# PEER value stage on one Trainium2 core: value unit and up-unit multiplied in turn, weights split in that order

## The chip, the cores and the metric

One Trainium2 chip, one of its cores. The metric is the device time of one execution in microseconds; the lower the better. TensorE does the matrix products, VectorE (DVE) and ScalarE (ACT) the elementwise work, GpSimd (POOL) a little of it, and the queue of SyncE (SP) starts the weight loads.

## What is computed

Two blocks of layers over 256 tokens of width 1024, all in float32. The change touches only the last part of each of the two layers of the second block, the PEER layer, a mixture of 16384 small experts:

```python
def peer_ffn(h, w_query, sub_keys, expert_u, expert_v):
    ...
    expert_idx = jnp.take_along_axis(cand_idx, pos, axis=-1)
    gates = jax.nn.softmax(best, axis=-1).astype(h.dtype)
    ...
    def block(args):
        xb, idx, g = args
        u = expert_u[idx]
        a = jax.nn.gelu(jnp.einsum('tkd,td->tk', u, xb)) * g
        return jnp.einsum('tk,tkd->td', a, expert_v[idx])
```

The kernel computes it densely: gelu(u·h) for all 16384 experts, times a gate matrix that is zero where an expert was not chosen, times v.

## The kernel before

**Tiles.** `expert_u` and `expert_v` are cut into 64 pairs each; a pair is one load of 1 MB and holds two units of 128 experts (128 partitions by 1024). An *up-unit* u(n,0), u(n,1) of pair n is multiplied by `project`: for each of 8 slices of 128 columns, three matmuls with the weight slice stationary and the 256 tokens moving (`triple`, L606 to L608), so 24 matmuls of 256 columns. A *value unit* v(n,0), v(n,1) takes 12 matmuls of 512 columns (`loose`, L611 to L613): stationary is a slice of the activation, moving is half of the weight unit; they add into four banks `acc[0..3]` over all 128 value units. There are three matmuls for each product because float32 is kept by splitting both factors: `w_hi` (rounded by ACT, L1145) and `w_lo = raw - w_hi` (by DVE, L1604), and likewise `p_hi` (ACT, L1539) and `p_lo` (DVE, L2176) for the activation.

**Buffers.** `raw` has three slots of one pair (NRAW = 3). `w_hi` and `w_lo` have four slots of one unit (NPAIR = 4): unit number g goes into slot g % 4, so ACT may split unit g only when TensorE has done unit g - 4 (semaphore `used`, in the trace a wait on L613 or L608). The numbers of the units follow `weight_order`, and every engine takes them in that order.

**Order.** NPAIRS = 33: when the value stage begins, 33 of the 64 up-pairs are done. Step n of the stage (n = 0..30) multiplies v(n,0), v(n,1) and then u(n+33,0), u(n+33,1); from n = 31 a step has value units only. In each step the other engines do, strictly in this order:
- ACT: gelu of up-pair n+32 (L1467, it frees a PSUM bank and needs the last up-unit of step n-1), `products(n+1)`, that is `p_hi` twice (L1539), every fourth step the load of a chunk of gates, and then four splits L1145.
- DVE: `products(n+1)`, that is the product with the gates (L2172, called the gate product below), which releases `p_hi`, and `p_lo` twice (L2176); then the four splits L1604.

```python
                        for e2 in range(2):
                            w_hi_upto(unit[("peer_v", l), 2 * n + e2] + NPAIR)
...
            def pair(key, n):
                w_hi_upto(unit[key, 2 * n + 1] + NPAIR)
```

With the unit numbers before, the four splits of step n are u(n+33,1), v(n+1,0), v(n+1,1), u(n+34,0). SP loads a pair when the last unit in its `raw` slot is split on DVE.

Of the kernel before, what the change touches and what calls it, by code (L numbers as in the profile page):

```python
# [17 lines left out]
T = 256  # L18
# [6 lines left out]
NRAW = 3  # L25
NPAIR = 4
# [85 lines left out]
def weight_order(a):  # L112

    order, first, n = [], {}, 0

    def add(key, src, count, lo="v", n0=0):
        nonlocal n
        for i in range(n0, n0 + count):
            first.setdefault(key, n) if n0 == 0 and i == 0 else None
            order.append((src[i], lo, n))  # L120
            place[key, 2 * i], place[key, 2 * i + 1] = n, n + 1
            n += 2

    place = {}
    for l in range(L):
        add(("ffn1_gu", l), a["ffn1_gu"][l], 22)
        add(("ffn1_down", l), a["ffn1_down"][l], 11)
        add(("w_in", l), a["w_in"][l], 8)
        add(("w_v", l), a["w_v"][l], 2)
        add(("w_out", l), a["w_out"][l], 4)  # L130
        add(("ffn2_gu", l), a["ffn2_gu"][l], 22)
        add(("ffn2_down", l), a["ffn2_down"][l], 11)
    spread, n_ada, seen = [], 0, 0
    for i, entry in enumerate(order):
        spread.append(entry)
        seen += not 33 <= i % 80 < 50
        while n_ada < 48 and n_ada < (seen - 2) * 48 // 122:
            spread.append((a["ada_w_2"][n_ada // 24][n_ada % 24], "ada", n_ada))
            n_ada += 1
    assert n_ada == 48  # L140
    order[:] = spread

    def add_peer(l):
        u, v = a["peer_u"][l], a["peer_v"][l]
        for i in range(8):
            add(("peer_q", l), a["peer_q"][l], 1, "v" if i < 2 else "p", i)
            if i >= 1:
                add(("peer_u", l), u, 1, "v" if i == 1 else "p", i - 1)
        add(("peer_u", l), u, NPOOL - 7, "p", 7)
        add(("peer_u", l), u, NPAIRS - NPOOL, "v", NPOOL)  # L150
        for i in range(64):
            add(("peer_v", l), v, 1, "v", i)
            if i + NPAIRS < 64:
                add(("peer_u", l), u, 1, "v", i + NPAIRS)

    add("ret_qk", a["ret_qk"], 8)
    add("ret_v", a["ret_v"], 8)
    add("ret_g", a["ret_g"], 8)
    add("ret_out", a["ret_out"], 8)
    add_peer(0)  # L160
    add("sgu_v", a["sgu_v"], 12)
    add("sgu_u", a["sgu_u"], 12)
    add("sgu_out", a["sgu_out"], 12)
    add_peer(1)
    return order, place, n


def build(nc, a, out):
    ctx = ExitStack()
    with ctx:  # L170
# [61 lines left out]
        hi_done = signal("w_hi_done", lambda n: n + 1)  # L232
        lo_count, ada_n, halves = {"v": 0, "p": 0}, 0, []
        lo_key = {}
        for k, (src, lo, n) in enumerate(order):
            for half in range(2):
                if lo == "ada":
                    halves.append((k, half, lo, 2 * n + half))
                else:
                    halves.append((k, half, lo, n + half))  # L240
                    lo_count[lo] += 1
                    lo_key[n + half] = (lo, lo_count[lo])
        w_lo_dve = signal("w_lo_done_dve", lambda n: lo_key[n][1])
        w_lo_pool = signal("w_lo_done_pool", lambda n: lo_key[n][1])
        lo_done = {"v": w_lo_dve, "p": w_lo_pool}
# [10 lines left out]
        class Banks:  # L256
# [3 lines left out]
            def take(self, key):  # L260
                self.at = (self.at + 1) % len(self.ids)
                i = self.ids[self.at]
                before, held[i] = held.get(i), key
                bank[key] = psum[i]
                return psum[i], before
# [336 lines left out]
        def _(e):  # L602
# [411 lines left out]
            def peer(l):  # L1014
# [14 lines left out]
                def u_pair(n):  # L1029
                    u_unit(2 * n)  # L1030
                    u_unit(2 * n + 1)
# [6 lines left out]
                def key_scores(n):  # L1038
# [7 lines left out]
                                         keys[:, 2 * n + z, :], start=True, stop=True)  # L1046
                    t.then_inc(psc_done.hit(l, n), 1)

                project_pairs(q, ("peer_q", l), 0, outs)
                for n in range(1, 8):  # L1050
                    if n > 1:
# [35 lines left out]
                for k in range(4):  # L1087
                    held[4 + k] = ("acc", l, k)
                w.wait_ge(*row_read(q))
                for n in range(64):  # L1090
                    for e2, ks in ((0, range(4)), (1, range(4))) if n < 63 else ((0, (0, 1)), (1, (0, 1)), (0, (2, 3)), (1, (2, 3))):
                        u = 2 * n + e2
                        g = unit[("peer_v", l), u]
                        wh, wl = weights(g)
                        i = u % 4
                        w.wait_ge(p_lo_done, p_lo_done(l, u))
                        for k in ks:
                            c, tt = slice(k // 2 * 512, (k // 2 + 1) * 512), slice(k % 2 * 128, (k % 2 + 1) * 128)
                            t = loose(acc[k], (p_hi[i][:, tt], p_lo[i][:, tt]), (wh[:, c], wl[:, c]), u == 0, u == 127)
                            if u == 127 and k < 3:  # L1100
                                t.then_inc(acc_done.hit(l, k), 1)
                        if ks[-1] == 3:
                            t.then_inc(used.hit(g), 1)
                    if n + NPAIRS < 64:
                        u_pair(n + NPAIRS)
                for m in range(KT):
                    if m % 2 == 0:
                        w.wait_ge(*free_after(held[m // 2]))
# [23 lines left out]
        def _(e):  # L1132
# [314 lines left out]
            def peer(l):  # L1447
# [97 lines left out]
                for n in range(64):  # L1545
                    if n < 63:
                        products(n + 1)
                        for e2 in range(2):
                            w_hi_upto(unit[("peer_v", l), 2 * n + e2] + NPAIR)
                    if n == 48:  # L1550
                        ready_root(3 + l)
                    if n + NPAIRS < 64:
                        u_pair(n + NPAIRS)
# [34 lines left out]
        def _(e):  # L1588
# [450 lines left out]
            def peer(l):  # L2039
# [140 lines left out]
                for n in range(64):  # L2180
                    if n < 63:
                        products(n + 1)
                        for e2 in range(2):
                            w_lo_upto(unit[("peer_v", l), 2 * n + e2] + NPAIR)
                    if n + NPAIRS < 64:
                        pair(("peer_u", l), n + NPAIRS)
                w.wait_ge(*unit_after(("peer_v", l), 127))
# [82 lines left out]
        @block.sync  # L2270
        def _(e):
            w = Waits(e)
            for k, (src, lo, n) in enumerate(order):
                if k == 0:
                    e.dma_start(raw_t[:, 0, 0:UNIT], src[:, 0:UNIT]).then_inc(raw_first.sem, 16)
                    e.dma_start(cols[:, 0:8], a["cols"][:, 0:8]).then_inc(loads["gain"].sem, 16)
                    w.wait_ge(raw_first, 16)
                    e.dma_start(raw_t[:, 0, UNIT:2 * UNIT], src[:, UNIT:2 * UNIT]).then_inc(landed[0].sem, 16)
                    continue
                if k < NRAW:  # L2280
                    w.wait_ge(*((loads["x2"], 16) if k == 1 else (landed[0], 16)))
                elif k >= NRAW:
                    _, before, m = order[k - NRAW]
                    if before == "ada":
                        w.wait_ge(ada_done, ada_done(2 * m + 1))
                    else:
                        w.wait_ge(lo_done[before], lo_key[m + 1][1])
                e.dma_start(raw_t[:, k % NRAW, :], src).then_inc(landed[k % NRAW].sem, 16)
                if k == 2:
                    e.dma_start(ident, a["ident"]).then_inc(loads["ident"].sem, 16)  # L2290
                    e.dma_start(iof, a["iota"]).then_inc(loads["iota"].sem, 16)
                    e.dma_start(crow, a["c_2"].partition_broadcast(128)).then_inc(loads["c"].sem, 16)
                    e.dma_start(relb, a["rel_bias"]).then_inc(loads["relb"].sem, 16)
                    e.dma_start(oh, a["onehot"]).then_inc(loads["oh"].sem, 16)
                    e.dma_start(anti, a["anti"]).then_inc(loads["anti"].sem, 16)
                    e.dma_start(half1, a["half1"]).then_inc(loads["half"].sem, 16)
                for l in range(L):
                    if n == unit[("peer_u", l), 2 * NPAIRS] and lo != "ada":
                        for i in range(2):
                            w.wait_ge(g_stored[i], 128 * (l + 1))  # L2300
                    for c in range(4):
                        if n == unit[("peer_u", l), 2 * (NPAIRS + c)] and lo != "ada":
                            e.dma_start(G[c], gates[l, :, :, c * 128:(c + 1) * 128].rearrange("g p c -> p g c")).then_inc(g_read[c].sem, 16)
            for m in range(KT):
                w.wait_ge(fin_ready, fin_ready(m))
                e.dma_start(out[:, m, :], fin[:, m, :]).then_inc(stored.sem, 16)
            w.wait_ge(stored, 16 * KT)
            w.wait_ge(bias_out, 16)
# [127 lines left out]
```

## Time and profile before

| | |
|---|---|
| median of 3 runs | 3047.86 us (3041.24 to 3049.73) |
| span of the profiled execution | 3041.1 us |
| TensorE busy | 3019.4 us, 99% of the span |
| DVE, ACT busy | 72%, 53% |
| granted clock of TensorE over the span | 0.997 |

The profile shows one execution, whose own time is given as its span; it lies 0.1 us under the fastest of the three runs and 6.8 us under their median. In the trace TensorE's matmuls overlap (each is shown for its whole way through the array), so the cost of one is the distance from its start to the next start, not its duration.

### The profile page before, as it was taken

How to read it: one execution, taken by the hardware profiler on the slowest of the kernel's cores; microseconds unless marked ns; L12 is line 12 of the kernel's file. 1: busy time of each engine (PE TensorE's matmuls, PEld its weight loads, DVE VectorE, ACT ScalarE, POOL GpSimd, SP SyncE). 2: the span in 40 equal slices, each digit the busy share in tenths (PEclk: the TensorE clock that was granted, in tenths of full speed). 3: DMA queues.
4: the chain of work that ended last, by engine and by line, in shares of the span. 5: the costliest groups of instructions: out<-in, count | busy, mean ns of one | idle time of the engine just before them, and what ended most of it. 6: DMA issues, size and time to landing. Idle time of an engine off the chain costs nothing.

```text
span 3041.1 us, 53499 instructions
## 1 busy us (share of the span) xinstructions
PE 3019.4 (99%) x22650; PEld 2849.6 (94%) x22650; DVE 2184.3 (72%) x3459; ACT 1615.1 (53%) x2399; POOL 255.2 (8%) x233
## 2 busy tenths in 40 slices
PE   9999999999999999999999999999999999999999
PEld 9998999999999999999999998889999999999887
DVE  6877787876788756899555557776679975555676
ACT  5565554565554455556544445556445564444554
POOL 0010001010001001820000000000146000000000
PEclk9999999999999999999999999999999999999999
DMA  7762577774277545557856667555445687666663
GB/s 258 267 248 96 195 277 256 273 275 167 102 258 290 173 146 180 178 180 291 296 206 214 216 212 245 208 190 191 163 170 181 229 302 249 218 213 216 222 235 125
DMA packets 153693, 654.61 MB, mean 215 GB/s; under 512 B 10508, under 2 KB 77648, under 8 KB 78960
## 3 DMA queue, kind: packets, MB, share of 16 engines
q1 hardware_dynamic: 97744, 584.99, 54.1%
q10 hardware_dynamic: 55296, 64.76, 6.3%
q8 instruction: 179, 2.93, 0.4%
q0 software_dynamic: 416, 1.45, 0.1%
q14 instruction: 58, 0.48, 0.0%
HBM read 616.55 MB, written 34.61 MB: 214 GB/s over the span
## 4 chain that ended last, share of the span: by engine, by line
PE 92%; DVE 6%; ACT 1%; issue 0%; DMA 0%; DVEq 0%; ACTq 0%
PE ps L606 18%; PE ps L607 18%; PE ps L608 18%; PE ps L612 8%; PE ps L613 8%; PE ps L611 8%; PE ps L1074 2%; PE ps L801 2%; DVE w_lo L1604 2%; PE ps L678 1%; PE ps L681 1%; PE ps L679 1%; PE ps L663 1%; PE ps L657 1%; PE ps L658 1%; PE ps L693 1%
## 5 line engine op out<-in xcount | busy, mean ns | idle before, releaser
L1604 DVE TENSOR_TENSOR w_lo<-raw,w_hi 128x1024 fp32r<-128x1024 f32 x933 | 1139.5, 1228 | 588.6 <-ACT w_hi L1145 587.6
L1145 ACT ACTIVATE w_hi<-raw 128x1024 fp32r<-128x1024 f32 x1000 | 1050.5, 1055 | 658.0 <-PE ps L608 357.1
L606 PE MATMUL ps<-h_hi,w_hi 128*128 128x256 f32 x4240 | 1188.6, 280 | 5.0 <-DVE w_lo L1604 3.4
L607 PE MATMUL ps<-h_lo,w_hi 128*128 128x256 f32 x4240 | 1179.1, 278 | 0.0
L608 PE MATMUL ps<-h_hi,w_lo 128*128 128x256 f32 x4240 | 1179.0, 278 | 0.0
L606 PEld LDWEIGHTS ps<-h_hi,w_hi 128*128 128x128 f32 x4240 | 797.1, 188 | 10.8 <-issue 4.1
L608 PEld LDWEIGHTS ps<-h_hi,w_lo 128*128 128x128 f32 x4240 | 802.2, 189 | 0.0
L607 PEld LDWEIGHTS ps<-h_lo,w_hi 128*128 128x128 f32 x4240 | 796.4, 188 | 2.8 <-issue 0.2
L613 PE MATMUL ps<-w_hi,at 128*128 128x512 f32 x1024 | 398.4, 389 | 0.0
L612 PE MATMUL ps<-w_lo,at 128*128 128x512 f32 x1024 | 398.4, 389 | 0.0
L611 PE MATMUL ps<-w_hi,at 128*128 128x512 f32 x1024 | 398.4, 389 | 0.0
L606 PE MATMUL ps<-at,w_hi 128*128 128x256 f32 x1024 | 284.2, 278 | 2.2 <-DVE w_lo L1604 1.8
L608 PE MATMUL ps<-at,w_lo 128*128 128x256 f32 x1024 | 283.7, 277 | 0.0
L607 PE MATMUL ps<-at,w_hi 128*128 128x256 f32 x1024 | 283.7, 277 | 0.0
L613 PEld LDWEIGHTS ps<-w_hi,at 128*128 128x128 f32 x1024 | 192.3, 188 | 39.7
L611 PEld LDWEIGHTS ps<-w_hi,at 128*128 128x128 f32 x1024 | 192.3, 188 | 37.5
L612 PEld LDWEIGHTS ps<-w_lo,at 128*128 128x128 f32 x1024 | 192.1, 188 | 37.6
L606 PEld LDWEIGHTS ps<-at,w_hi 128*128 128x128 f32 x1024 | 192.9, 188 | 2.9 <-issue 2.0
L608 PEld LDWEIGHTS ps<-at,w_lo 128*128 128x128 f32 x1024 | 192.4, 188 | 0.0
L607 PEld LDWEIGHTS ps<-at,w_hi 128*128 128x128 f32 x1024 | 192.2, 188 | 0.0
L2244 POOL TENSOR_TENSOR tmp_h<-x 128x256 f32<-128x256 f32 x50 | 36.8, 736 | 1842.0 <-DVE x L1649 1717.8
L1467 ACT ACTIVATE at<-ps 128x512 f32<-128x512 f32 x128 | 76.7, 599 | 201.5 <-PE ps L608 201.5
(287 smaller groups left out, 3210.6 us busy)
## 6 DMA issues: line engine op xcount, KB each, us to landing
raw<-in_peer_u SPq DMA_DIRECT2D x128, 1024.0 KB, 4.8
raw<-in_peer_v SPq DMA_DIRECT2D x128, 1024.0 KB, 4.8
raw<-in_ffn_gu SPq DMA_DIRECT2D x87, 1024.0 KB, 4.9
raw<-in_ada_w SPq DMA_DIRECT2D x48, 1024.0 KB, 5.1
raw<-in_ffn_down SPq DMA_DIRECT2D x44, 1024.0 KB, 4.9
gates<-at ACTq DMA_DIRECT2D x32, 1024.0 KB, 4.9
at<-gates ACTq DMA_DIRECT2D x24, 1024.0 KB, 6.0
raw<-in_w_in SPq DMA_DIRECT2D x16, 1024.0 KB, 4.9
```

Of the source, the lines that this page charges most:

```text
L606: e.matmul(o, lhs[0], rhs[0], start=start, stop=False)
L607: e.matmul(o, lhs[0], rhs[1], start=False, stop=False)
L608: return e.matmul(o, lhs[1], rhs[0], start=False, stop=stop)
L611: e.matmul(o, lhs[0], rhs[0], start=start, stop=False, skip_group_check=True)
L612: e.matmul(o, lhs[0], rhs[1], start=False, stop=False, skip_group_check=True)
L613: return e.matmul(o, lhs[1], rhs[0], start=False, stop=stop, skip_group_check=True)
L801: t = e.matmul(conv.bank[:, i * T:(i + 1) * T], mdiag[:, n, :], mu_[:, 2 + i, k:k + T], start=k == 0, stop=k == 30)
L1074: t = e.matmul(b[:, k * 128:(k + 1) * 128], Ah[j][:, z, :, 4 * i + k], Bh[j][:, 2 * i + k // 2, :, k % 2], start=z == 0, stop=z == 1)
L1145: e.activation(whi[:, u % NPAIR, :], raw(k, half), ACT.Copy).then_inc(hi_done.hit(u), 1)
L1467: e.activation(R[:, i:i + 2, :].rearrange("p a b -> p (a b)"), bank["u", l, n], ACT.Gelu_apprx_tanh).then_inc(u_done.hit(l, n), 1)
L1604: e.tensor_tensor(wlo[:, m % NPAIR, :], raw(k, half), whi[:, m % NPAIR, :].bitcast(FP), ALU.subtract).then_inc(w_lo_dve.hit(m), 1)
L2244: t = e.tensor_tensor(one if m else total, x[:, m, :], x[:, m, :], ALU.mult)
```

## The change

In steps 0 to 30 a value unit and an up-unit of the same half are multiplied in turn: `values_and_unit(n, e2)` issues one matmul of 512 columns, two of 256, and so on, 12 and 24 of them; then the same for the other half. The units are numbered v(n,0), u(n+33,0), v(n,1), u(n+33,1), and are split in that order. Steps 31 to 63 stay. The matmuls are the same in number and shape. The load of a pair now waits for the split of the unit two numbers after the pair's first (`m + last`).

```diff
+    def add_two(key, src, i, key2, src2, i2):
+        nonlocal n
+        for z, (ky, s, j) in enumerate(((key, src, i), (key2, src2, i2))):
+            order.append((s[j], "v", n + z, 2))
+            place[ky, 2 * j], place[ky, 2 * j + 1] = n + z, n + z + 2
+        n += 4
...
-        for i in range(64):
-            add(("peer_v", l), v, 1, "v", i)
-            if i + NPAIRS < 64:
-                add(("peer_u", l), u, 1, "v", i + NPAIRS)
+        for i in range(64 - NPAIRS):
+            add_two(("peer_v", l), v, i, ("peer_u", l), u, i + NPAIRS)
+        add(("peer_v", l), v, 64 - (64 - NPAIRS), "v", 64 - NPAIRS)
...
+                def values_and_unit(n, e2):
+                    v, u = 2 * n + e2, 2 * (n + NPAIRS) + e2
+                    gv, gu = unit[("peer_v", l), v], unit[("peer_u", l), u]
+                    i, s = v % 4, slice(e2 * T, (e2 + 1) * T)
+                    if e2 == 0:
+                        u_bank[0] = take(ub, ("u", l, n + NPAIRS))
+                    o = u_bank[0][:, s]
+                    vh, vl = weights(gv)
+                    w.wait_ge(p_lo_done, p_lo_done(l, v))
+                    uh, ul = weights(gu)
+                    for k in range(4):
+                        c, tt = slice(k // 2 * 512, (k // 2 + 1) * 512), slice(k % 2 * 128, (k % 2 + 1) * 128)
+                        a_, b_ = 2 * k, 2 * k + 1
+                        ca, cb = slice(a_ * 128, (a_ + 1) * 128), slice(b_ * 128, (b_ + 1) * 128)
+                        e.matmul(acc[k], p_hi[i][:, tt], vh[:, c], start=v == 0, stop=False, skip_group_check=True)
+                        e.matmul(o, uh[:, ca], hh_[:, a_, :], start=k == 0, stop=False, skip_group_check=True)
+                        e.matmul(o, uh[:, ca], hl_[:, a_, :], start=False, stop=False, skip_group_check=True)
+                        e.matmul(acc[k], p_hi[i][:, tt], vl[:, c], start=False, stop=False, skip_group_check=True)
+                        e.matmul(o, ul[:, ca], hh_[:, a_, :], start=False, stop=False, skip_group_check=True)
+                        e.matmul(o, uh[:, cb], hh_[:, b_, :], start=False, stop=False, skip_group_check=True)
+                        t = e.matmul(acc[k], p_lo[i][:, tt], vh[:, c], start=False, stop=False, skip_group_check=True)
+                        if k == 3:
+                            t.then_inc(used.hit(gv), 1)
+                        e.matmul(o, uh[:, cb], hl_[:, b_, :], start=False, stop=False, skip_group_check=True)
+                        t = e.matmul(o, ul[:, cb], hh_[:, b_, :], start=False, stop=k == 3, skip_group_check=True)
+                    t.then_inc(used.hit(gu), 1)
...
-                for n in range(64):
+                for n in range(64 - NPAIRS):
+                    for e2 in range(2):
+                        values_and_unit(n, e2)
+                for n in range(64 - NPAIRS, 64):
...
-                        for e2 in range(2):
-                            w_hi_upto(unit[("peer_v", l), 2 * n + e2] + NPAIR)
+                        if n + NPAIRS >= 64:
+                            w_hi_upto(unit[("peer_v", l), 2 * n + 1] + NPAIR)
...
-                        w.wait_ge(lo_done[before], lo_key[m + 1][1])
+                        w.wait_ge(lo_done[before], lo_key[m + last][1])
```

On TensorE, at the first value step of the first PEER layer, the rows before are these (`ps1` is the bank of the up-pair, `ps4` to `ps7` are `acc`, the `at` tiles are `p_hi` and `p_lo`):

```order
L606 MATMUL ps0<-h_hi,w_hi 128x256
L607 MATMUL ps0<-h_lo,w_hi 128x256
L608 MATMUL ps0<-h_hi,w_lo 128x256
L611 MATMUL ps4<-w_hi,at29456_229_230 128x512 [waits n_scaled,w_lo_done_dve,G_ready,p_lo_done]
L612 MATMUL ps4<-w_lo,at29456_229_230 128x512
L613 MATMUL ps4<-w_hi,at30480_237_238 128x512
L611 MATMUL ps5<-w_hi,at29456_229_230 128x512
L612 MATMUL ps5<-w_lo,at29456_229_230 128x512
```

and with the change these, ending where the second half's group begins:

```order
L1074 MATMUL ps7<-w_hi,at29456_229_230 128x512
L1075 MATMUL ps1<-h_hi,w_hi 128x256
L1076 MATMUL ps1<-h_lo,w_hi 128x256
L1077 MATMUL ps7<-w_lo,at29456_229_230 128x512
L1078 MATMUL ps1<-h_hi,w_lo 128x256
L1079 MATMUL ps1<-h_hi,w_hi 128x256
L1080 MATMUL ps7<-w_hi,at30480_237_238 128x512
L1083 MATMUL ps1<-h_lo,w_hi 128x256
L1084 MATMUL ps1<-h_hi,w_lo 128x256
L1074 MATMUL ps4<-w_hi,at29712_231_232 128x512 [waits w_lo_done_dve,p_lo_done]
```

A group of 36 matmuls has one wait at its head, for the split of both of its units, where before each unit waited for its own. The value unit's slot is given back by L1080, the third matmul from the group's end, and the up-unit's by the last.

On ACT, one whole step before (gelu, `p_hi` twice, four splits, the next gelu):

```order
L1467 ACTIVATE at12544_225_226<-ps0 128x512 [waits p_lo_done,w_used]
L1539 ACTIVATE at29968_233_234<-at12544_225_226 128x256 [waits rg_mul]
L1539 ACTIVATE at30224_235_236<-at12544_225_226 128x256
L1145 ACTIVATE w_hi<-raw 128x1024
L1145 ACTIVATE w_hi<-raw 128x1024 [waits w_used,raw_landed2]
L1145 ACTIVATE w_hi<-raw 128x1024 [waits w_used]
L1145 ACTIVATE w_hi<-raw 128x1024 [waits w_used,raw_landed0]
L1467 ACTIVATE at12544_225_226<-ps1 128x512 [waits p_lo_done,w_used]
```

and the same step with the change:

```order
L1506 ACTIVATE at12544_225_226<-ps0 128x512 [waits p_lo_done,w_used]
L1578 ACTIVATE at29968_233_234<-at12544_225_226 128x256 [waits rg_mul]
L1578 ACTIVATE at30224_235_236<-at12544_225_226 128x256
L1184 ACTIVATE w_hi<-raw 128x1024
L1184 ACTIVATE w_hi<-raw 128x1024 [waits w_used,raw_landed2]
L1184 ACTIVATE w_hi<-raw 128x1024 [waits w_used,raw_landed0]
L1184 ACTIVATE w_hi<-raw 128x1024 [waits w_used]
L1506 ACTIVATE at12544_225_226<-ps1 128x512 [waits p_lo_done,w_used]
```

The four splits were u(n+33,1), v(n+1,0), v(n+1,1), u(n+34,0) and are now u(n+33,1), v(n+1,0), u(n+34,0), v(n+1,1): the wait for a new up-pair (`raw_landed0`) moves one place forward, and the last split before gelu is that of a value unit of the second half.

DVE's rows are the same in both, with the four splits in the new order of units:

```order
L2211 TENSOR_TENSOR at12544_225_226<-at12544_225_226,at4096_273_274 128x512 [waits u_done]
L2215 TENSOR_TENSOR at30992_241_242<-at12544_225_226,at29968_233_234 128x256 [waits p_hi_done]
L2215 TENSOR_TENSOR at31248_243_244<-at12544_225_226,at30224_235_236 128x256 [waits p_hi_done]
L1643 TENSOR_TENSOR w_lo<-raw,w_hi 128x1024 [waits w_hi_done] x4
L2211 TENSOR_TENSOR at12544_225_226<-at12544_225_226,at6144_275_276 128x512 [waits g_read3,u_done]
```

The last of the four splits (`x4`), now v(n+1,1), stands ahead of the next gate product in this queue.

## Rows read from the trace of the kernel before

**Rows 1.** The page: span, busy time by engine, chain that ended last.

```profile
span 3041.1 us, 53499 instructions
PE 3019.4 (99%) x22650; PEld 2849.6 (94%) x22650; DVE 2184.3 (72%) x3459; ACT 1615.1 (53%) x2399; POOL 255.2 (8%) x233
...
PE 92%; DVE 6%; ACT 1%; issue 0%; DMA 0%; DVEq 0%; ACTq 0%
```

**Rows 2.** Busy time, clock and DMA share of a value step.

```profile
core 0: us, PE busy (x) PEld busy (x) DVE busy (x) ACT busy (x) POOL busy (x), PEclk, DMA share, GB/s
1688.50:1699.59 11.09, 11.09 (x74) 10.15 (x73) 6.26 (x8) 5.34 (x7) 0.00 (x0) 1.00 0.86 283
```

**Rows 3.** Timeline of TensorE, one value step: start, us, what.

```profile
1499.93 0.39 PE L611 MATMUL ps<-w_hi,at 128*128 128x512 f32 x1
...
1505.37 0.28 PE L606 MATMUL ps<-h_hi,w_hi 128*128 128x256 f32 x1
1505.49 0.28 PE L607 MATMUL ps<-h_lo,w_hi 128*128 128x256 f32 x1
...
1511.03 0.39 PE L611 MATMUL ps<-w_hi,at 128*128 128x512 f32 x1
```

**Rows 4.** Timeline of TensorE ahead of the value stage, up-units alone.

```profile
1461.07 0.28 PE L606 MATMUL ps<-h_hi,w_hi 128*128 128x256 f32 x1
...
1466.51 0.28 PE L606 MATMUL ps<-h_hi,w_hi 128*128 128x256 f32 x1
```

**Rows 5.** Timeline of TensorE, end of a value unit.

```profile
1604.98 0.39 PE L613 MATMUL ps<-w_hi,at 128*128 128x512 f32 x1
1605.21 0.28 PE L606 MATMUL ps<-h_hi,w_hi 128*128 128x256 f32 x1
```

**Rows 6.** Timeline of ACT, one value step.

```profile
1599.97 0.60 ACT L1467 ACTIVATE at<-ps 128x512 f32<-128x512 f32 x1 [1.71 <-PE ps L608]
1600.16 0.37 ACTq L1514 DMA_DIRECT2D at<-gates  x1
1600.46 0.71 ACT L1539 ACTIVATE at<-at 128x256 fp32r<-128x256 f32 x2
1601.08 1.05 ACT L1145 ACTIVATE w_hi<-raw 128x1024 fp32r<-128x1024 f32 x1
...
1605.41 1.06 ACT L1145 ACTIVATE w_hi<-raw 128x1024 fp32r<-128x1024 f32 x1 [1.60 <-PE ps L613]
```

**Rows 7.** Timeline of DVE, the same step.

```profile
1602.16 1.23 DVE L1604 TENSOR_TENSOR w_lo<-raw,w_hi 128x1024 fp32r<-128x1024 f32 x1 [0.49 <-ACT w_hi L1145]
...
1606.50 1.23 DVE L1604 TENSOR_TENSOR w_lo<-raw,w_hi 128x1024 fp32r<-128x1024 f32 x1 [1.43 <-ACT w_hi L1145]
1609.39 1.23 DVE L1604 TENSOR_TENSOR w_lo<-raw,w_hi 128x1024 fp32r<-128x1024 f32 x1 [1.66 <-ACT w_hi L1145]
1610.53 0.68 DVE L2172 TENSOR_TENSOR at<-at,at 128x512 f32<-128x512 f32 x1
```

**Rows 8.** Timelines of DVE and ACT just ahead of and in the first value step.

```profile
1473.25 0.69 DVE L2172 TENSOR_TENSOR at<-at,at 128x512 f32<-128x512 f32 x1 [1.10 <-DMA at<-gates]
...
1480.38 1.22 DVE L1604 TENSOR_TENSOR w_lo<-raw,w_hi 128x1024 fp32r<-128x1024 f32 x1 [0.50 <-ACT w_hi L1145]
...
1473.97 0.73 ACT L1539 ACTIVATE at<-at 128x256 fp32r<-128x256 f32 x2 [0.88 <-DVE at L2172]
```

**Rows 9.** Timeline of TensorE, a restart after a wait for a split.

```profile
12.80 0.39 PE L606 MATMUL ps<-h_hi,w_hi 128*128 128x256 f32 x1 [0.60 <-DVE w_lo L1604]
13.03 0.28 PE L607 MATMUL ps<-h_lo,w_hi 128*128 128x256 f32 x1
```

**Rows 10.** Timeline of SP's queue, and the time to landing of loads.

```profile
1603.42 0.33 SPq L2288 DMA_DIRECT2D raw<-in_peer_v  x1
...
raw<-in_peer_u SPq DMA_DIRECT2D x6, 1024.0 KB, 4.8
...
raw<-in_peer_u SPq DMA_DIRECT2D x3, 1024.0 KB, 6.0
...
DMA to landing us min/median/max: 4.7/5.7/7.5
```

**Rows 11.** Waits: steps 0 to 30, then the steps of value units alone.

```profile
DVE w_lo L1604 <- ACT w_hi L1145: 125.2, 124, 1.7
ACT w_hi L1145 <- PE ps L613: 68.5, 62, 1.6
...
ACT at L1539 <- DVE at L2172: 57.2, 31, 1.9
```

More of the change, by code:

```diff
@@ L119, in add @@
             first.setdefault(key, n) if n0 == 0 and i == 0 else None
-            order.append((src[i], lo, n))
+            order.append((src[i], lo, n, 1))
             place[key, 2 * i], place[key, 2 * i + 1] = n, n + 1
             n += 2
+    def add_two(key, src, i, key2, src2, i2):
[4 more added lines that the diff above has]
+        n += 4
     place = {}
@@ L137, in weight_order @@
         while n_ada < 48 and n_ada < (seen - 2) * 48 // 122:
-            spread.append((a["ada_w_2"][n_ada // 24][n_ada % 24], "ada", n_ada))
+            spread.append((a["ada_w_2"][n_ada // 24][n_ada % 24], "ada", n_ada, 1))
             n_ada += 1
@@ L234, in build @@
         lo_key = {}
-        for k, (src, lo, n) in enumerate(order):
-            for half in range(2):
+        for k, (src, lo, n, apart) in enumerate(order):
+            if apart == 2 and order[k - 1][3] == 2 and order[k - 1][2] == n - 1:
+                continue
+            for k_, half in ((k, 0), (k, 1)) if apart == 1 else ((k, 0), (k + 1, 0), (k, 1), (k + 1, 1)):
                 if lo == "ada":
-                    halves.append((k, half, lo, 2 * n + half))
+                    halves.append((k_, half, lo, 2 * n + half))
                 else:
-                    halves.append((k, half, lo, n + half))
+                    m = order[k_][2] + half * apart
+                    halves.append((k_, half, lo, m))
                     lo_count[lo] += 1
-                    lo_key[n + half] = (lo, lo_count[lo])
+                    lo_key[m] = (lo, lo_count[lo])
         w_lo_dve = signal("w_lo_done_dve", lambda n: lo_key[n][1])
@@ L1103, in peer @@
                             t.then_inc(used.hit(g), 1)
-                    if n + NPAIRS < 64:
-                        u_pair(n + NPAIRS)
                 for m in range(KT):
@@ L2182, in peer @@
                         products(n + 1)
-                        for e2 in range(2):
-                            w_lo_upto(unit[("peer_v", l), 2 * n + e2] + NPAIR)
+                        if n + NPAIRS >= 64:
+                            w_lo_upto(unit[("peer_v", l), 2 * n + 1] + NPAIR)
                     if n + NPAIRS < 64:
@@ L2272, in _ @@
             w = Waits(e)
-            for k, (src, lo, n) in enumerate(order):
+            for k, (src, lo, n, apart) in enumerate(order):
                 if k == 0:
@@ L2282, in _ @@
                 elif k >= NRAW:
-                    _, before, m = order[k - NRAW]
+                    _, before, m, last = order[k - NRAW]
                     if before == "ada":
```

## The prediction

> **What bounds the kernel now.** I read the page first: TensorE is busy for 99% of the span, and the chain that ended last runs over it for 92% [rows 1]. So a microsecond saved or lost on TensorE is one of the whole time, and other engines matter only where they make it wait. Next, the table of a stretch, for one value step: 11.09 us, TensorE busy all of it at granted clock 1.00, which is its upper level of 2.4 GHz, with DVE busy 6.26 and ACT 5.34 us [rows 2]. The table of waits for steps 0 to 30 has DVE waiting for ACT's splits (125.2 us) and ACT for the slots (68.5 us), and no line with TensorE as the one that waits [rows 11]. The reader is to see that nothing makes TensorE wait there, and that both helpers have some 5 us of slack *per step*. Whether they still have it *per half step* is the question of this change.
>
> Then the timeline of TensorE. The first value matmul of a step starts at 1499.93, the first of the up-units at 1505.37, the next step at 1511.03 [rows 3]. So 24 matmuls of 512 columns take 5.44 us, 226.7 ns each, and 48 of 256 columns take 5.66 us, 117.9 ns each. Ahead of the stage the same kind of up-unit matmul runs faster: 48 of them from 1461.07 to 1466.51, 113.3 ns each, exactly half of a 512 [rows 4]. In the value stage the 256s therefore pay 4.6 ns each beyond what their columns cost, and the 512s pay nothing. There are 48 x 31 x 2 = 2976 such matmuls in the two layers: 13.7 us, 0.45% of the time. That is all that another order of matmuls can win.
>
> **The change: the matmuls.** Count and shapes stay. Mixed, a 256 follows a 512 or a 256, and a 512 follows a 256. Of these neighbours the trace shows both: the first 256 behind a 512 takes 0.12 us (1505.37 to 1505.49 [rows 3]), as the others do. The second 256 of each two has a 256 before it, whatever comes after. I see no neighbourhood in the new order that the old one has not already shown at 117.9, so I take 117.9 and 226.7, and keep 113.3 as the lower bound. A group of 12 and 24 then lasts 2.72 + 2.83 = 5.55 us, or 5.44 at the lower bound. For an added cost of the alternation there is no row; between the two speeds of a 256 lie 4.6 ns, and as much again on each would be the same 13.7 us the other way.
>
> The Trainium skill (TensorE: Matmul & The Clock Gate, section "Back-to-back issue gap") gives a warm gap of N/2.4 + 2.5 ns that depends on the moving size alone, 109.2 ns for 256 and 215.8 for 512. Both are below the rows (117.9 or 113.3, and 226.7), so as a price it fails here; as a rule it says that the order of shapes changes nothing, and a pure reordering would by it be worth 0 us.
>
> **The change: the splits.** This is where I expect the time to go. A slot of w_hi and w_lo is given back only at the end of a unit. Before, the units ended one after another, about 2.8 us apart, and each split had the time of three other units to be done. Now value unit and up-unit of a half run together and end together, and both units of the *second* half of step n must be split in the 5.55 us of its first half, in slots that were in use until the step before ended. ACT and DVE take work in fixed order, so this is a chain. I set 0 at the start of step n and add it up:
> - The last value matmul of the group before, which frees the slot of v(n,1), has two 256s and itself ahead of the boundary: it starts at -(0.23 + 0.24) = -0.46.
> - From such a start to ACT's split: 1604.98 to 1605.41 [rows 5, 6], +0.43, so -0.03.
> - ACT's split to DVE's split of the same unit: 1605.41 to 1606.50 [rows 6, 7], +1.09: 1.06.
> - Behind it in DVE's queue stands the gate product of pair n+1: 1609.39 to 1610.53 [rows 7], +1.14, and its 0.68: 2.88. Before the change this place had the split of an up-unit whose slot came back 2.83 us earlier, so it was over when gelu began.
> - p_hi waits for that product: 1473.25 + 0.69 to 1473.97 [rows 8], +0.03: 2.91. Gelu is long done by then.
> - Two p_hi, which stand ahead of the split of u(n+33,1) in ACT's queue: 1600.46 to 1601.08 [rows 6], +0.62: 3.53.
> - That split, and DVE's share behind it: 1601.08 to 1602.16 [rows 6, 7], +1.08, and 1.23 more: 5.84. The two p_lo in between take less than ACT's split and lie beside it.
> - TensorE sees it (+0.03 as elsewhere) and restarts: the first matmul behind a wait for w_lo takes 0.23 instead of 0.12 [rows 9], so 0.1 more: 5.97.
>
> The first half's group is over at 5.55. TensorE waits 0.42 us in the middle of the step, effective restart included. The second half then starts at 5.97 and lasts 5.55: the step takes 11.52 instead of 11.09. If the 256s ran at 113.3, the group would end at 5.44, but the chain would not be shorter (it hangs on the end of the *previous* group), so the step would be 5.98 + 5.44 = 11.42, still 0.33 longer.
>
> It is missing in step 0: the slot of v(0,1) is free early, and the split of u(33,1) already ends there at 1480.38 + 1.22 = 1481.60, 3.95 us into the stage [rows 8], before 5.55. That leaves steps 1 to 30 of two layers, 60 waits. Sum: 60 x 0.42 = **25 us**, on the span of 3041.1: 3066.
>
> The other edits. The raw slot of pair v(n) comes back when v(n,1) is split, at 1.06 + 1.23 = 2.29, and 0.03 later, as at 1603.42, SP loads u(n+34) into it: 4.8 us to landing, 6.0 beside a load of gates [rows 7, 10]. It is there at 7.1 to 8.3; then 1.1 and 1.2 us of splits, done by 10.7, needed at 11.52. Hidden, with 0.8 us to spare. The load that follows it starts at 5.87 and is needed a step later. The gate load in ACT's queue is issued while p_hi runs (1600.16 for 0.37 us, against 1601.08 for the next split [rows 6]) and stays behind it: nothing. Steps 31 to 63 keep their order; their waits of ACT for the gate product, 57.2 us in 31 [rows 11], show that p_hi does hang on DVE's queue when a value unit is the last split, with no harm there because no up-unit is due. In steps 0 to 30 no such wait is among the longest before.
>
> **The rivals.**
> - *A, the chain and fast 256s.* For it: they run at 113.3 elsewhere. Against: behind every 512 here they start slow. The sum is 60 x 0.33 = 20, less the 2 first steps' 0.4: 3060.
> - *B, the other side: the chain fits, and the 256s run at 113.3.* The load of weights for a 256 would hide behind the 512 before it, and the gain is the full 13.7 us: 3027. It decides if the chain is 0.53 us shorter than I add up (5.97 against 5.44), about a third of DVE's split; every link of it is a row of this trace, so I think that unlikely.
> - *C, the change does nothing.* TensorE stays at 226.7 and 117.9 and the chain is shorter by 0.42 us: 3041.
> - *D, the chain and a late load.* Beside a load of gates a weight load has taken up to 7.5 us [rows 10]: 2.32 + 7.5 + 2.4 = 12.2 against 11.5, 0.7 us in 10 steps of each layer, 14 us more; about as much comes from an alternation that costs 4.6 ns a matmul. 3080; with both 3094.
>
> **How the numbers follow.** Chances: the chain as added up 0.58, A 0.13, D 0.13 (all slower by over 0.3%), C 0.09, B 0.07. 0.3% is about what a measurement of this kernel tells from no change. The median of the runs lies 6.8 us above the profiled span; added to it the forecast is 3047.9 + 25 = 3073, a ratio of 1.008. On that basis A gives 3067, D 3087 to 3101, C 3048, B 3034. The likeliest case alone spans 3064 to 3081 (0.1 us of error in the chain is 6 us). The range for 8 in 10 reaches from just under that, 3057, to 3091. Slower by over 0.3% has 0.58 + 0.13 + 0.13 = 0.84, less a little for a chain that is only half as late: 0.82. Within 0.3%: 0.11. Faster: 0.07.
>
> **What will show it.** In the profile after: one stall of TensorE per value step, at the head of the second half's group, ended by DVE's split of an up-unit, 60 in all. A matmul is shown for its whole 0.28 us, so the idle time shown is only 0.1 to 0.2 us; the distance from the last start of the group to the next start is 0.44 instead of 0.12. Also a step of 11.4 to 11.6 us; ACT's p_hi waiting for DVE's gate product in steps 0 to 30; starts of the 256s 118 ns apart. I am wrong if the waits are absent (a link is shorter, or the queue order differs from what I read), if they stand at the *first* half's group (then it is the load), or if the 256s run at 113.

## The result

The changed kernel takes 3082.7 us (median of 4 runs, 3082.3 to 3086.6) against 3046.5 us before (3041.2 to 3049.7): the ratio is 1.0126, with a 95% interval of 1.0114 to 1.0138. It is slower by 36 us. I had forecast 25 us slower and a range of 3057 to 3091, so the direction and the range hold, and the size is a third short.

### The profile page after: what moved, and what is told of

Read it like the earlier page. It is cut to its first block, busy times and chain, and to the rows that moved or that the text cites. A ratio compares the mean times of both kernels' runs of the same rounds, so it can differ in the third digit from the quotient of the medians.

```text
span 3080.5 us, 53497 instructions
## 1 busy us (share of the span) xinstructions
PE 3049.6 (99%) x22650; PEld 2858.1 (93%) x22650; DVE 2182.6 (71%) x3459; ACT 1614.3 (52%) x2399; POOL 255.5 (8%) x233
## 4 chain that ended last, share of the span: by engine, by line
PE 80%; DVE 11%; ACT 6%; issue 1%; DMA 1%; SPq 0%; DVEq 0%; ACTq 0%
PE ps L616 14%; PE ps L618 14%; PE ps L617 14%; DVE w_lo L1643 6%; PE ps L621 4%; PE ps L622 4%; PE ps L623 4%; ACT w_hi L1184 4%; PE ps L1074 2%; PE ps L1112 2%; PE ps L1080 2%; PE ps L1077 2%; PE ps L811 2%; ACT at L1578 1%; PE ps L688 1%
## 5 line engine op out<-in xcount | busy, mean ns | idle before, releaser
L616 PE MATMUL ps<-h_hi,w_hi 128*128 128x256 f32 x3248 | 909.2, 280 | 4.1 <-DVE w_lo L1643 3.5
L617 PE MATMUL ps<-h_lo,w_hi 128*128 128x256 f32 x3248 | 899.8, 277 | 0.0
L618 PE MATMUL ps<-h_hi,w_lo 128*128 128x256 f32 x3248 | 899.6, 277 | 0.0
L616 PEld LDWEIGHTS ps<-h_hi,w_hi 128*128 128x128 f32 x3248 | 611.5, 188 | 7.4 <-issue 4.7
L618 PEld LDWEIGHTS ps<-h_hi,w_lo 128*128 128x128 f32 x3248 | 611.6, 188 | 0.0
L617 PEld LDWEIGHTS ps<-h_lo,w_hi 128*128 128x128 f32 x3248 | 611.0, 188 | 0.4 <-issue 0.2
L1074 PE MATMUL ps<-w_hi,at 128*128 128x512 f32 x496 | 203.0, 409 | 9.5 <-DVE w_lo L1643 9.5
L621 PE MATMUL ps<-w_hi,at 128*128 128x512 f32 x528 | 205.4, 389 | 0.0
L623 PE MATMUL ps<-w_hi,at 128*128 128x512 f32 x528 | 205.4, 389 | 0.0
L1578 ACT ACTIVATE at<-at 128x256 fp32r<-128x256 f32 x256 | 92.8, 410 | 203.8 <-DVE at L2211 203.8
L1080 PE MATMUL ps<-w_hi,at 128*128 128x512 f32 x496 | 198.4, 400 | 0.0
```

The costliest lines, as they stand in the source:

```text
L616: e.matmul(o, lhs[0], rhs[0], start=start, stop=False)
L617: e.matmul(o, lhs[0], rhs[1], start=False, stop=False)
L618: return e.matmul(o, lhs[1], rhs[0], start=False, stop=stop)
L621: e.matmul(o, lhs[0], rhs[0], start=start, stop=False, skip_group_check=True)
L623: return e.matmul(o, lhs[1], rhs[0], start=False, stop=stop, skip_group_check=True)
L1074: e.matmul(acc[k], p_hi[i][:, tt], vh[:, c], start=v == 0, stop=False, skip_group_check=True)
```

## The profile after, beside that of before

The profiled execution spans 3080.5 us, 39.4 more than before. From its page:

```profile
span 3080.5 us, 53497 instructions
PE 3049.6 (99%) x22650; PEld 2858.1 (93%) x22650; DVE 2182.6 (71%) x3459; ACT 1614.3 (52%) x2399; POOL 255.5 (8%) x233
...
PE 80%; DVE 11%; ACT 6%; issue 1%; DMA 1%; SPq 0%; DVEq 0%; ACTq 0%
```

TensorE is still busy for 99%, which alone would tell nothing. The chain that ended last tells more: TensorE's share fell from 92 to 80% [rows 1], DVE's rose from 6 to 11 and ACT's from 1 to 6. Part of the time now hangs on the splits. The same table of one value step as in [rows 2]:

```profile
1595.66:1607.39 11.73, 11.57 (x74) 10.28 (x73) 6.26 (x7) 5.34 (x8) 0.00 (x0) 1.00 0.52 180
```

The step takes 11.73 us instead of 11.09, DVE and ACT work as long as before (6.26 and 5.34 us), the clock is at the same level, and only 0.16 us of TensorE is idle. So a quarter of the loss is plain to see, and the rest is in matmuls whose starts are further apart. The timeline of TensorE at both halves' heads (start us, us, what) shows it:

```profile
1595.18 0.40 PE L1080 MATMUL ps<-w_hi,at 128*128 128x512 f32 x1
1595.42 0.28 PE L1083 MATMUL ps<-h_lo,w_hi 128*128 128x256 f32 x1
1595.54 0.28 PE L1084 MATMUL ps<-h_hi,w_lo 128*128 128x256 f32 x1
1595.66 0.40 PE L1074 MATMUL ps<-w_hi,at 128*128 128x512 f32 x1
...
1601.22 0.28 PE L1084 MATMUL ps<-h_hi,w_lo 128*128 128x256 f32 x1
1601.66 0.47 PE L1074 MATMUL ps<-w_hi,at 128*128 128x512 f32 x1 [0.16 <-DVE w_lo L1643]
1601.97 0.28 PE L1075 MATMUL ps<-h_hi,w_hi 128*128 128x256 f32 x1
...
1607.39 0.40 PE L1074 MATMUL ps<-w_hi,at 128*128 128x512 f32 x1
```

Two things are new against [rows 3]. The first half has no wait at its head (0.12 us from L1084 to L1074 at 1595.54), the second has one: 0.44 us from 1601.22 to 1601.66, ended by DVE's w_lo, and the first 512 behind it takes 0.31 to the next start. It stands 30 times in each layer, at every second half but the first. And a 512 takes 0.24 us from its start to the next (1595.18 to 1595.42), where it took 0.227. Over steps 0 to 30 the starts are 239 ns apart for a 512 (the first behind a wait left out) and 117.0 for a 256; before it was 226.7 and 117.8.

The chain of splits can be read off in the timelines of ACT and of DVE in the same step:

```profile
1595.62 1.06 ACT L1184 ACTIVATE w_hi<-raw 128x1024 fp32r<-128x1024 f32 x1 [3.53 <-PE ps L1080]
1596.59 0.58 ACT L1506 ACTIVATE at<-ps 128x512 f32<-128x512 f32 x1
1598.58 0.72 ACT L1578 ACTIVATE at<-at 128x256 fp32r<-128x256 f32 x2 [1.41 <-DVE at L2211]
1599.21 1.04 ACT L1184 ACTIVATE w_hi<-raw 128x1024 fp32r<-128x1024 f32 x1
...
1602.85 1.06 ACT L1184 ACTIVATE w_hi<-raw 128x1024 fp32r<-128x1024 f32 x1 [0.43 <-DMA raw<-in_peer_u]
```

```profile
1596.71 1.23 DVE L1643 TENSOR_TENSOR w_lo<-raw,w_hi 128x1024 fp32r<-128x1024 f32 x1 [3.37 <-ACT w_hi L1184]
1597.86 0.69 DVE L2211 TENSOR_TENSOR at<-at,at 128x512 f32<-128x512 f32 x1
...
1600.29 1.23 DVE L1643 TENSOR_TENSOR w_lo<-raw,w_hi 128x1024 fp32r<-128x1024 f32 x1 [0.50 <-ACT w_hi L1184]
```

ACT idles 3.53 us for the slot of the value unit, and then everything comes at once: split (ACT), split (DVE), gate product (DVE), p_hi (ACT, which waited for it 1.41 us), split, split. Both engines have 5 us to spare in the step. But from 1595.62 to 1601.52 the links of this chain follow each other with 0.04 us or less between them, so the slack of one engine in this half is of no use: it idles only while the other works on the chain.

## The experiments

My theory after this look had two causes, the chain of splits (a wait of 0.32 us and 0.07 us more for the first matmul behind it, 60 times, 23 us) and a 512 that alternates with 256s (12 ns more, 1488 times, 18 us, less 2 us on the 256s). Together they make the 39 us of the span. The first four kernels separate the two.

**The up-unit's split ahead of the gate product.** On ACT and on DVE alike:

```diff
                 for n in range(64):
+                    if n + NPAIRS < 64:
+                        w_hi_upto(unit[("peer_u", l), 2 * (n + NPAIRS) + 1] + 1)
                     if n < 63:
                         products(n + 1)
```

> The changed kernel, but ACT and DVE split u(n+33,1) ahead of products(n+1) in steps 0 to 30; all else stays. Theory (the wait of 0.32 us and the slow restart of 0.07 us at the head of each second half come from the chain of v(n,1) split, gate product, p_hi, split of u(n+33,1)): the 60 waits vanish, the step falls from 11.73 to 11.35 us, and the time falls by 60 x 0.39 = 23 us, to a span of about 3057. What is left over before, 16 us, is then the matmuls: 512s start to start 239 ns, 256s 117. Rival 1 (the 512s are slow because TensorE was stopped in every step): without the waits they return to 227 ns, span about 3041. Rival 2 (the wait is for a load): it stays, span 3080.

Measured: ratio to before 1.0039 (1.0023 to 1.0056), span 3054.2 us. In the timeline of TensorE the head of a half looks like this everywhere:

```profile
1607.53 0.28 PE L1084 MATMUL ps<-h_hi,w_lo 128*128 128x256 f32 x1
1607.64 0.40 PE L1074 MATMUL ps<-w_hi,at 128*128 128x512 f32 x1
1607.88 0.28 PE L1075 MATMUL ps<-h_hi,w_hi 128*128 128x256 f32 x1
...
1613.33 0.40 PE L1074 MATMUL ps<-w_hi,at 128*128 128x512 f32 x1
```

No wait is left: no start in steps 0 to 30 of either layer is over 0.24 us behind the one before. A half takes 1613.33 - 1607.64 = 5.69 us, a step 11.36. The wait did come from the order in the queues, with the same loads, slots and work. And the 512s stay at 239 ns, so their slowness does not come from the stops (rival 1 falls), nor the stops from a load (rival 2 falls). From the first value matmul of a layer to its last the trace has 523.2 us before, 542.7 with the change and 531.5 here: of the 19.5 us that a layer lost, the chain is worth 11.2 and the matmuls 8.3. The span is 3 us under what I expected, and the value stages are not: the rest of the span takes 1991.3 us here, 1994.7 before and 1995.2 with the change. Over the ten kept traces that rest lies between 1990 and 1998 us (the stage taken from the first matmul of its step 0), so below I go by the length of the stages.

**The same splits, the matmuls not mixed.** The body of `values_and_unit` makes two lists and merges them by a pattern; here the pattern is

```diff
-                    for k in range(4):
-                        ...
+                    for z in "v" * 12 + "u" * 24:
```

> The changed kernel with its numbering, its order of splits and its joint wait, but in each half the 12 value matmuls come first and then the 24 of the up-unit. Theory: both causes are gone. The value unit's slot is free 2.83 us before the half ends, so the chain is over early, and nothing alternates: 227 and 118 ns, step 11.09 us, span 3041, same as before. Rival (the order of splits, or the joint wait, costs by itself): waits stay at the head of the second half, step over 11.4, span over 3060.

Measured: ratio 1.000 (0.9989 to 1.0010), span 3039.8 us; a group takes 5.547 us, and the value stages last 523.2 us as before. The numbering, the order of splits and the joint wait cost nothing by themselves. They cost time only with a value unit's slot that comes back late.

**Unmixed, but with the value unit last.** The pattern is `"u" * 23 + "v" * 12 + "u"`.

> The changed kernel, but in each half 23 matmuls of the up-unit, then the 12 of the value unit, then the last of the up-unit: the value unit's slot is freed as late as in the change, nothing alternates. Theory: the chain of splits stays and is seen alone. It starts 0.11 us later than in my prediction's sum, so the second half starts at 6.08 instead of 5.97 us, the step takes 6.08 + 5.55 = 11.63, the time is 60 x 0.54 = 32 us over before: span 3073. 512s at 227 ns. Rival (the slow 512s come from the late splits or the waits, not from the alternation): 512s at 239 here too, step 11.7 or more, span 3080 or more.

Measured: ratio 1.0125 (1.0106 to 1.0144), span 3080.5 us: as slow as the change itself, with 512s at 227 ns in most places. The timeline of TensorE at the head of a second half:

```profile
1499.64 0.28 PE L1086 MATMUL ps<-h_hi,w_lo 128*128 128x256 f32 x1
1500.32 0.36 PE L1086 MATMUL ps<-h_hi,w_hi 128*128 128x256 f32 x1 [0.40 <-DVE w_lo L1646]
1500.52 0.28 PE L1086 MATMUL ps<-h_lo,w_hi 128*128 128x256 f32 x1
```

0.68 us from start to start, where 0.12 is the rule. The second half starts at 6.11 us in all 60 steps (expected 6.08). In the second layer the step then takes 11.67 (expected 11.63). In the first layer it takes 11.73 on average, for a reason that the second half shows: behind all 30 stops of the second layer the 256s run at 113 ns, behind those of the first only 11 times, else at 118. The 512s that come first behind these 256s (three, in a third of the first layer's halves nine) average 231 to 235 ns, the others take 227. The two stages are 36 us longer than before. So the chain alone, begun 0.11 us later than in the change, can make the kernel as slow as the change. The rival falls as the cause in the change: most 512s here run at 227 beside 60 waits, and with the early split they ran at 239 with none. But the others show that a stop can make a few 512s slow without any alternation, which I had not expected. The chain's cost and the matmuls' don't simply add: what hangs on the end of the previous group is not made worse by a longer group beside it.

**Six orders, one kernel.** This and the next two kernels were run once each and are read from their traces alone. On the kernel with the early split, the order within a half changes from step to step by n % 6 (v is a matmul of 512 columns of the value unit, u one of 256 of the up-unit).

> As the kernel with the early split of u(n+33,1), but with another order in each step, by n % 6: 0 v u u twelve times; 1 vvv and six u, four times; 2 v u v u u u six times; 3 vv and four u, six times; 4 twelve v, then 24 u; 5 six v and twelve u, twice. Read from the starts of matmuls by step. A group without any cost of alternation takes 12 x 226.7 + 24 x 117.9 = 5.55 us; in the change it took 5.67. Theory 1 (a single 512 between two 256s is slow, by 12 ns): only orders 0 and 2 are slow, 5.67 and 5.67, the others 5.55. Theory 2 (each switch of size costs about 5 ns): 5.68, 5.59, 5.68, 5.61, 5.56, 5.57. Rival (it is the share of 256s, whatever the order): all 5.67.

Measured, from the starts of matmuls in the trace, as medians of the second halves (us a group; mean ns of a 512 and of a 256):

```
0  v u u, twelve times            5.600   234.2  116.9   (5.680 in step 0, on 239)
1  vvv and six u, four times      5.547   226.7  117.7
2  v u v u u u, six times         5.600   231.3  117.6
3  vv and four u, six times       5.560   232.1  115.7
4  twelve v, 24 u                 5.547   226.7  117.8
5  six v and twelve u, twice      5.547   226.7  117.7
```

Theory 1 is nearest (a lone 512 is the slow one), though it had 5.67 for orders 0 and 2; theory 2 and the rival fall: order 1 switches eight times in a group, and its second halves cost nothing. But the row for order 0 was a surprise. The same order took 5.680 in step 0 and 5.600 in the steps that followed order 5. Order 2 likewise took 5.67 instead of 5.60 in the one half that came behind a stop (second layer, step 2). The speed of a matmul depends on what ran before, not on its neighbours alone. In order 3 some 256s ran at 113 ns.

**Other operands.** The alternation once more, with operands exchanged in sets of 6 steps; from the second set on the kernel no longer computes the layer, only its matmuls' shapes and count are kept.

> As the kernel with the early split of u(n+33,1), v u u throughout, but in runs of 6 steps with other operands, which leave the computation of the layer wrong: steps 0 to 5 (and 30) as it is; 6 to 11 the up-unit's stationary operand is read from p_hi and p_lo instead of w_hi and w_lo; 12 to 17 the value unit's stationary operand is read from w_hi and w_lo instead of p_hi and p_lo; 18 to 23 the up-unit's moving operand is a part of the value unit's weights instead of h; 24 to 29 the up-unit's matmuls write into the banks of the value unit. Group as it is: 5.68 us, 512s at 239 ns. Theory 1 (only the alternation of sizes counts): 5.60 to 5.68 in all of them. Theory 2 (a weight load from w_hi or w_lo slows a 512 that streams from the same tensors): steps 6 to 11 fall to 5.55, steps 12 to 17 stay or rise. Theory 3 (turning between PSUM banks): steps 24 to 29 fall to 5.55.

Measured: 5.680 us a group in all sets but one, with 512s at 239 ns: with the 256s' weights from p_hi and p_lo, with the 512s' weights from w_hi and w_lo, and with all output in the same banks. Theories 2 and 3 fall. With the 256s' moving operand from the weights it took 5.633, 512s at 233 ns. That lies in theory 1's range, but it is a difference that the sizes alone don't make; I have no account of it.

**Rows of 256s behind one, two or three 512s.** Sets of 5 steps each, with the early split.

> As the kernel with the early split of u(n+33,1), every half with all its 36 matmuls, but in runs of 5 steps with another order: steps 0 to 4 vv uuuu vv, 19 u, 8 v, u; 5 to 9 vv, 23 u, 10 v, u; 10 to 14 v, 23 u, 11 v, u; 15 to 19 vvv, 23 u, 9 v, u; 20 to 24 vv uuuu twice, vv, 15 u, 6 v, u; 25 to 29 12 v, 24 u. Theory (a 256 runs at 118 or at 113 ns by what went before, and one or two 512s between 256s put the following ones onto 113): a long row of u behind vv runs at 113, so steps 5 to 9 and 15 to 19 take 5.47 to 5.50 us a group, and 0 to 4 likewise, against 5.547 in steps 25 to 29. Rival (each row of u behind a 512 runs at 118, however many 512s there are): all at 5.55 or above.

Measured, medians of a group in us, in the order of the steps: 5.507, **5.487**, 5.580, 5.613, 5.527, 5.547. The theory holds where two 512s stand between 256s and fails for one and for three: their 256s stay at 117.8 ns, and the group of three is 0.07 us longer than unmixed, where I expected 5.47 to 5.50. The timeline of TensorE in step 7, behind `u v v`:

```profile
1553.72 0.28 PE L1086 MATMUL ps<-h_hi,w_lo 128*128 128x256 f32 x1
1553.84 0.40 PE L1082 MATMUL ps<-w_hi,at 128*128 128x512 f32 x1
1554.08 0.40 PE L1082 MATMUL ps<-w_lo,at 128*128 128x512 f32 x1
1554.31 0.28 PE L1086 MATMUL ps<-h_hi,w_hi 128*128 128x256 f32 x1
1554.43 0.28 PE L1086 MATMUL ps<-h_lo,w_hi 128*128 128x256 f32 x1
1554.54 0.28 PE L1086 MATMUL ps<-h_hi,w_lo 128*128 128x256 f32 x1
1554.66 0.28 PE L1086 MATMUL ps<-h_hi,w_hi 128*128 128x256 f32 x1
...
1555.79 0.28 PE L1086 MATMUL ps<-h_lo,w_hi 128*128 128x256 f32 x1
```

From 1554.66 to 1555.79 there are ten matmuls, 113 ns each, the speed of [rows 4] in the middle of the value stage. The two 512s cost 0.24 and 0.23 us, a little more than alone, and the row of 23 gains it back.

**The whole stage in that order.** The pattern of steps 5 to 9, `"vv" + "u" * 23 + "v" * 10 + "u"`, in all 31 steps, with the early split.

> As the kernel with the early split of u(n+33,1), but in every half of steps 0 to 30: vv, 23 u, 10 v, u, which took 5.487 us a group in five steps of the kernel of runs, against 5.547 for 12 v and 24 u. Theory (two 512s between 256s put the 256s behind them onto 113 ns): no waits, 124 groups x 0.060 = 7.4 us under before, span about 3033, ratio 0.9976. Rival (it holds only for some steps): span 3036 to 3041.

Measured: ratio 0.9974 (0.9964 to 0.9984), span 3031.8 us; a value stage lasts 519.5 us instead of 523.2, which is 7.4 us for both, as expected.

**The kernel before with one matmul moved.** Its own splits and units; one 256 of the up-pair is issued two 512s early, so that the last two 512s stand between 256s.

```diff
+                        for p, x in enumerate(row):
+                            if e2 == 1 and p == 10:
+                                ...
+                                e.matmul(b[:, 0:T], uh[:, 0:128], hh_[:, 0, :], start=True, stop=False, skip_group_check=True)
+                            t = e.matmul(*x, start=n == 0 and e2 == 0 and p % 3 == 0, stop=False, skip_group_check=True)
```

> The kernel before, with its order of splits and units, and one edit: in steps 0 to 30 the first matmul of the up-pair is issued ahead of the last two of the second value unit (22 v, u, v v, 47 u). Theory: the 47 behind vv run at 113 instead of 118, less some 45 ns at the switches: step 10.93 instead of 11.09 us, 62 x 0.17 = 10 us, span about 3031, ratio 0.9966. Rival (the row of 47 falls back to 118 on its way, or the gain is eaten at the next value unit): step 11.0 or more, span 3036 or more.

Measured: ratio 0.9961 (0.9947 to 0.9974), span 3029.7 us; a value stage lasts 518.0 us, the shortest here, which is 10.3 us for both. By the ratios alone it can't be told from the version before. One step of it in the timeline of TensorE:

```profile
1603.80 0.28 PE L1107 MATMUL ps<-h_hi,w_hi 128*128 128x256 f32 x1
1603.91 0.40 PE L1108 MATMUL ps<-w_lo,at 128*128 128x512 f32 x1
1604.15 0.40 PE L1108 MATMUL ps<-w_hi,at 128*128 128x512 f32 x1
1604.39 0.28 PE L1116 MATMUL ps<-h_lo,w_hi 128*128 128x256 f32 x1
...
1614.72 0.28 PE L1107 MATMUL ps<-h_hi,w_hi 128*128 128x256 f32 x1
```

The step takes 10.92 us against 11.09 (expected 10.93), with every matmul of before in it.

## Why the prediction was right, and where it was short

- **The bound and what an order can win.** Right. TensorE sets the time, and the 4.6 ns that a 256 pays in the stage are real and can be had: two kernels got 7 and 10 us of the 13.7 in their value stages. The change got 2 us of it; its 256s run at 117.0.
- **The chain of splits.** Right, link by link. With the start of the step at 1595.66, the sum gave and the trace has: freeing matmul -0.46 and -0.48; ACT's split -0.03 and -0.04; DVE's split 1.06 and 1.05; end of the gate product 2.88 and 2.89; p_hi 2.91 and 2.92; ACT's split of the up-unit 3.53 and 3.55; end of DVE's 5.84 and 5.86. Moving one split ahead on ACT and DVE removed all 60 waits, and so did giving the value unit's slot back early; that shows the cause.
- **The restart of TensorE.** Short by 0.1 us. I took 0.03 us from DVE's end to TensorE; that is the step between ACT and DVE. Here it is 0.14 to the first matmul (1601.52 to 1601.66), most of it ahead of its weight load, which starts at 1601.63. The 0.1 us that I added for the restart was sized by the distance from first to second start; measured there it is 0.07, and it comes on top. 60 x 0.1 = 6 us. The trace of before could have told me. It has two kinds of restart behind DVE's split, and [rows 9] show the rarer one (0.05 us to the first start, then 0.22 to the next). Of ten such stops in it, seven are like this one, with 0.15 and then 0.19:

```profile
863.52 1.22 DVE L1604 TENSOR_TENSOR w_lo<-raw,w_hi 128x1024 fp32r<-128x1024 f32 x1
...
864.89 0.36 PE L606 MATMUL ps<-h_hi,w_hi 128*128 128x256 f32 x1 [0.43 <-DVE w_lo L1604]
...
865.08 0.28 PE L607 MATMUL ps<-h_lo,w_hi 128*128 128x256 f32 x1
```

- **The matmuls, the term that was mis-sized.** "I see no neighbourhood in the new order that the old one has not already shown" was the step that failed. Each pair of neighbours had been shown, the succession of three had not: 256, 512, 256. The 512s cost 239 instead of 226.7 ns and the group 0.13 us more. As the first half's share is swallowed by the wait, one of the two groups of a step counts: 60 x 0.13 = 8 us. With the 25 forecast and the 6 above it makes the 39 of the span. I had put this price only into rival D, "an alternation that costs 4.6 ns a matmul"; by its size (133 ns in 36 matmuls, 3.7 ns each) that is what came true, beside the chain.
- **The rule of one gap for each size.** From the formula of the Trainium skill (TensorE: Matmul & The Clock Gate, section "Back-to-back issue gap") I concluded that the order of shapes changes nothing. That was more than the section says: it gives the formula for an isolated matmul, and for a stream of weight loads and matmuls it says that both set the distance, with 131 ns for 512 columns. These traces have 226.7, 234 and 239 ns for 512 columns and 113.3 and 117.9 for 256, at the same granted clock 1.00. They agree neither with the formula nor with the 131 ns, and my conclusion is refuted.
- **The late load** of rival D did not come. The up-pair's load is seen on ACT's split at 1602.85, 7.19 us into the step (I had 7.1 to 8.3), and the first halves start without a wait in all steps.
- **Rivals A, B and C** fall: the 256s of the change run at 117.0 and not 113.3 ns, and there are 60 waits. In B, 0.53 us is 0.43 of DVE's split of 1.23, not a third; nothing hangs on it.

What stays open is why TensorE has these speeds. It is not the tensors that the weights come from nor the banks, but the 256s' moving operand has a share in it (512s at 233 instead of 239). A succession is kept up once begun (256s at 113 or 118, single 512s at 231, 234 or 239 on average) and is changed by some disturbances, such as `u v v u` or a stop, and not by others, such as `u v u` or `u v v v u`. A stop does not always change it: with the value unit last, 30 of 30 in the second layer put the 256s on 113 and only 11 of 30 in the first. No run here tells by what mechanism.

## What to carry to other kernels

When two streams of work are mixed, look at when their buffers come back, not only at the sums: here four slots that were freed one by one came back in twos, and engines with 5 us of slack in 11 were late by 0.3 to 0.4 us. Walk one period of each in-order queue from the event that frees the buffer, and place what is needed first ahead of what is needed later; that alone recovered 22 of 39 us in the value stages. And where a rate differs between two stages for the same instruction, try small changes of order and read starts, not durations: one matmul moved by two places gained 10 us, where the whole rearrangement had lost 36.

## What the runs showed of the hardware that I had not expected

- In steady rows a matmul of 256 columns takes 113.3 or 117.9 ns from start to start at the same granted clock, with the same operands, and stays with either for the whole row of 48 in the stage; its shown duration tells which (0.276 or 0.281 us).
- A single 512 between 256s takes 228 to 240 ns, again by what ran before (239 in the change), against 226.7 inside a row of its own.
- Two 512s between 256s put the row of 256s behind them onto 113.3 ns within four matmuls, in every one of the 124 and 62 places where it was used; one or three do not.
- A stop of TensorE that ends with DVE's split costs 0.14 us from DVE's end to the first start, and 0.07 us more on that matmul, in all 60 places of the change. Elsewhere in the traces some stops have 0.05 us and then 0.11 more; what picks the kind is open.
